# A decoder step with a mixture of experts: filled slots only, two-deep expert buffers, PLE weights split during the expert tiles

## The reference

```
xn = rmsnorm(h, g_ffn)
# top-1 of 4 groups, top-2 of its 8 experts, 32 experts in all
hg = silu(xn @ w_gate[e]) * (xn @ w_up[e])      # 1024 -> 256
y  = sum over the token's two experts of weight * (hg @ w_down[e])
h  = h + y
h  = h + sigmoid(rmsnorm(h, g_ple) @ w_ple_gate) * (p @ w_ple_proj)
out = rmsnorm(h, g_final)
```

## Time and profile before

| what | value |
|---|---|
| median of 3 runs | 1182.15 us (1180.9 to 1182.17) |
| profiled execution, span from first to last instruction | 1182.7 us |
| PE busy | 1075.1 us, 91% |
| DVE, ACT, POOL busy | 45%, 27%, 24% |
| DMA moved | 219.93 MB, mean 186 GB/s |
| gate/up matmuls, L1839 | 264.9 us busy |
| down matmuls, L1850 | 133.2 us busy |

### The profile page before, as it was taken

How to read it: one execution, slowest core, us unless ns; L and a number is a source line. 1 busy time by engine, 2 the same in 40 slices (tenths; PEclk the granted TensorE clock), 3 DMA queues, 4 the chain that set the end, 5 groups by cost and what they waited for, 6 DMA issues and landing times.

```text
span 1182.7 us, 13729 instructions
## 1 busy us (share of the span) xinstructions
PE 1075.1 (91%) x4696; PEld 573.2 (48%) x4696; DVE 534.8 (45%) x678; ACT 319.1 (27%) x573; POOL 279.3 (24%) x287
## 2 busy tenths in 40 slices
PE   4899979999999789995299999999999999589996
PEld 3556535555555555553144444444444444244442
DVE  6169856777765864344511211112111121356663
ACT  7342223222234433231011111111111111335553
POOL 0577235566415211110110100101010010232200
PEclk9999989989998799997599999999999999889998
DMA  7446610000004312228369999999999897743311
GB/s 254 129 154 219 131 4 1 1 0 0 0 1 124 113 44 99 71 71 308 114 253 360 370 369 366 375 363 369 370 359 380 328 350 275 255 125 116 115 45 58
DMA packets 50425, 219.93 MB, mean 186 GB/s; under 512 B 13569, under 2 KB 14866, under 8 KB 40146
## 3 DMA queue, kind: packets, MB, share of 16 engines
q1 hardware_dynamic: 42466, 190.58, 44.7%
q0 software_dynamic: 7920, 28.84, 7.3%
HBM read 180.44 MB, written 38.96 MB: 186 GB/s over the span
## 4 chain that ended last, share of the span: by engine, by line
PE 75%; DVE 11%; DMA 5%; ACT 3%; issue 2%; POOL 1%; DVEq 1%; SPq 0%; ACTq 0%; POOLq 0%
PE psum L1839 21%; PE psum L1614 12%; PE psum L1850 10%; PE psum L1925 8%; PE psum L1757 8%; DVE arena L1194 6%; PE psum L1830 3%; PE psum L1915 2%; DMA arena<-in_w_gu 2%; PE psum L1799 1%; PE psum L1681 1%; PE psum L1680 1%; PE psum L1790 1%; PE psum L1684 1%; PE psum L1669 1%
## 5 line engine op out<-in xcount | busy, mean ns | idle before, releaser
L1839 PE MATMUL psum<-arena 128*128 128x512 f32 x592 | 264.9, 601 | 4.0 <-DMA arena<-in_w_gu 2.8
L1194 DVE SCALAR_TENSOR_TENSOR arena<-arena,wc x120 | 185.3, 1544 | 17.4 <-DVE arena L1194 17.0
L1839 PEld LDWEIGHTS psum<-arena 128*128 128x128 f32 x592 | 111.1, 193 | 131.7 <-issue 126.4
L1614 PE MATMUL psum<-arena 128*128 128x512 f16 (+1 forms) x864 | 153.7, 332 | 0.6 <-ACT arena L887 0.6
L1850 PE MATMUL psum<-arena 128*128 128x512 f32 x296 | 133.2, 593 | 1.0 <-DVE arena L1488 1.0
L1484 DVE TENSOR_TENSOR arena<-arena,psum 128x256 f32<-128x256 f32 x37 | 15.6, 421 | 249.0 <-ACT arena L1057 211.5
L1614 PEld LDWEIGHTS psum<-arena 128*128 (+1 forms) x864 | 68.3, 98 | 78.6 <-issue 9.5
L1606 PE MATMUL psum<-arena 128*128 128x384 f16 x576 | 96.8, 332 | 4.0 <-DVE arena L1161 2.4
L1757 PE MATMUL psum<-arena 128*128 128x512 f16 x432 | 98.7, 386 | 0.8 <-DVE arena L1322 0.8
L1925 PE MATMUL psum<-arena 128*128 128x512 f16 x432 | 96.5, 383 | 2.5 <-DVE arena L1543 2.5
L787 POOL COPY idx<-ids 128x1 int32 (+1 forms) x32 | 6.3, 196 | 322.0 <-PE psum L1830 262.6
(11 more groups left out here) (232 smaller groups left out, 1231.1 us busy)
## 6 DMA issues: line engine op xcount, KB each, us to landing
arena<-in_w_gu SPq DMA_DIRECT2D x37, 2048.0 KB, 8.6
arena<-in_w_dn SPq DMA_DIRECT2D x37, 1024.0 KB, 10.5
yrows<-arena SPq DMA_DIRECT2D x37, 512.0 KB, 3.5
yrows<-PT SPq DMA_DIRECT2D x2, 4096.0 KB, 19.4
side<-in_w_tok SPq DMA_DIRECT2D x16, 388.0 KB, 3.4
arena<-in_x SPq DMA_DIRECT2D x9, 512.0 KB, 4.2
side<-in_x SPq DMA_DIRECT2D x9, 512.0 KB, 4.0
xn<-arena SPq DMA_DIRECT2D x9, 512.0 KB, 2.9
```

The source lines that it names most:

```text
L1194: dve.scalar_tensor_tensor(acc, src, w[:, k:k + 1], acc, ALU.mult, ALU.add).then_inc(conv, 1)
L1614: x = pe.matmul(out, xnT[w][:, k, bass.ds(n * P, P)], wtok[m][:, k, col:col + width], start=k + w + m == 0, stop=k == KC - 1 and w == 1)
L1839: x = pe.matmul(psum[:, 2 + sl, :], xgT[sl][:, k, :], wgu[sl][:, k, :], start=k == 0, stop=k == KC - 1)
```

## The change

- `experts` takes a second function `between`, called after tiles 0 to 3 and 28 to 31; tiles 4 to 27 run in a loop of two.
- Weights, gathered rows, transposed rows and results have two buffers instead of three. Gate/up comes in two halves with a semaphore each. SP asks for gate/up of t+2 when gate_up(t) is done and for down of t behind that.
- The one-hot matmul carries token+1, negative for a second choice, so that an empty slot shows as 0. DVE makes `ids` and `idsY` from it; an empty slot's index is out of bounds and its row is left out (slot 0 of an empty tile keeps an index, to a spare row). The gather buffers are cleared once by POOL.
- POOL gathers four tiles ahead in its list and scatters results with an indirect DMA straight to row token + m x 1152 of `yrows`. SP then loads result rows directly (`load_y`) instead of POOL gathering them.
- Only the 64 padding rows of each half of `yrows` are zeroed, not the extra tiles.
- The eight chunks of the PLE gate weight are loaded and split after tiles 0 to 3 and 28 to 31.
- Many small tiles move to one scratch tensor `tmp`, part of which is reused by these weights and results.

The diff, cut to its core:

```diff
-    put("token", token * (token < SEQ + NS))
+    put("token", (token + 1) * (token < SEQ + NS))
+    put("empty", np.concatenate([np.where(s == 0, TOK - 1, NOROW), np.where(s == 0, 2 * TOK, NOROW)], 1) + 1)
...
+def experts(eng, body, between):
+
+
+    for t in range(NE):
+        if t == 4:
+            with eng.Fori(2, NE // 2 - 2) as i:
+                body(2 * i, 0)
+                body(2 * i + 1, 1)
+        elif not 4 <= t < NE - 4:
+            body(t, t % 2)
+            between(t if t < 4 else t - NE + KC)
...
-    return t // 3 if isinstance(t, int) else (t - s) // 3
-
-
-def extra_turn(t, s):
-
-    return 16 * ((NE + 2 - s) // 3) + 8 * (t - (2 - s)) + 16
+    return 8 * (t - s) + 16
...
+        wgu = [at(R3 + 4096 * j, KC, 2 * FF) for j in range(2)]
+        wdn = [at(R4 + 2048 * j, FC, D) for j in range(2)]
+        xg = [at(R3 + 8192, D), at(R4 + 4096, D)]
+        xgT = [at(RT + D * j, KC, P) for j in range(2)]
+        yt = [tat(D * j, D) for j in range(2)]
+        sil = [at(RT + 2048 + FF * j, FF) for j in range(2)]
+        hg = at(RT + 2048 + 2 * FF, FF)
+        hT = at(RT + 2048 + 3 * FF, FC, P)
...
+        wple = at(R1 + 8192, D)
+        wgate = [thalves(2048 + D * k, 1, D) if k < 4 else halves(R5 + D * (k - 4), 1, D) for k in range(KC)]
...
             sp.wait_ge(zero, 1)
-            for half in range(2):
-                sp.dma_start(a["yrows"][NE * P:NTILE * P, half * 512:(half + 1) * 512].rearrange("(t p) w -> p t w", p=P),
-                             PT[:].rearrange("p a b -> p (a b)").unsqueeze(1).to_broadcast([P, EXTRA, 512])
-                             ).then_inc(y_zero, 16)
+            for m in range(2):
+                sp.dma_start(a["yrows"][m * TOK + SEQ + NS:(m + 1) * TOK].rearrange("p (a b) -> p a b", b=512),
+                             PT[0:TOK - SEQ - NS].rearrange("p a b -> p (a b)").unsqueeze(1)
+                             .to_broadcast([TOK - SEQ - NS, 2, 512])).then_inc(y_zero, 16)
...
+            def load_gu(t, sl):
+                for u in range(2):
+                    if late(t, 2):
+                        sp.wait_ge(gu_ps, t - 1)
+                    sp.dma_start(wgu[sl][:, 4 * u:4 * u + 4, :], a["w_gu"][bass.ds(t, 1), :, 4 * u:4 * u + 4, :]
+                                 .rearrange("a p k f -> (a p) k f")).then_inc(gu_in[sl][u], 16)
+
+            def load_dn(t, sl):
+                if late(t, 2):
+                    sp.wait_ge(y_ps, t - 1)
                 sp.dma_start(wdn[sl], a["w_dn"][bass.ds(t, 1)].rearrange("a p k f -> (a p) k f")).then_inc(dn_in[sl], 16)
...
             sp.wait_ge(og_rdy, NT)
-            weights(1, 1)
+            load_gu(0, 0)
             xn2_store(NT - 1, 0)
-            sp.wait_ge(w_ps, 2 * NT)
-            weights(0, 0)
+            load_gu(1, 1)
             sp.wait_ge(lg_ps, NT)
-
+            load_dn(0, 0)
+            load_dn(1, 1)
...
+            def load_ple(k):
+                if k:
+                    sp.wait_ge(wl_lo, KC + k)
+                sp.dma_start(wple, a["w_ple"][:, k]).then_inc(wple_in, 16)
 
             def expert_io(t, sl):
-                y_store(t, sl)
-                weights(t + 3, sl)
-
-            with sp.Fori(0, (NE - 5) // 3) as i:
-                for sl in range(3):
-                    expert_io(3 * i + sl, sl)
-            expert_io(NE - 5, 0)
-            expert_io(NE - 4, 1)
-            y_store(NE - 3, 2)
+                if not isinstance(t, int) or t < NE - 2:
+                    load_gu(t + 2, sl)
+                else:
+                    with sp.If(count > t + 2 - NE):
+                        extra_gu(t + 2 - NE, sl)
+                if late(t, 2):
+                    load_dn(t, sl)
+
+            def extra_gu(t, sl):
+                e = sp.value_load(plan[0:1, bass.ds(t, 1)], min_val=0, max_val=NE - 1)
+                for u in range(2):
+                    sp.wait_ge(gu_ps, t + NE - 1)
+                    sp.dma_start(wgu[sl][:, 4 * u:4 * u + 4, :], a["w_gu"][bass.ds(e, 1), :, 4 * u:4 * u + 4, :]
+                                 .rearrange("a p k f -> (a p) k f")).then_inc(gu_in[sl][u], 16)
+
+            def extra_io(t, sl):
+                e = sp.value_load(plan[0:1, bass.ds(t, 1)], min_val=0, max_val=NE - 1)
+                sp.wait_ge(y_ps, t + NE - 1)
+                sp.dma_start(wdn[sl], a["w_dn"][bass.ds(e, 1)].rearrange("a p k f -> (a p) k f")).then_inc(dn_in[sl], 16)
+                with sp.If(count > t + 2):
+                    extra_gu(t + 2, sl)
+                hold(sp, passed)
...
+            experts(sp, expert_io, load_ple)
             extra(sp, count, extra_io)
-            for sl in range(3):
-                sp.wait_ge(y_out[sl], 16 * ((NE + 2 - sl) // 3))
-            sp.sem_inc(y_all, 1)
+
+            def load_y(n, j):
+                if late(n, 2):
+                    sp.wait_ge(add_rdy, 2 * n - 2)
+                for m in range(2):
+                    sp.dma_start(yg[j][m], a["yrows"][bass.ds(n * P + m * TOK, P), :]).then_inc(yg_in[j][m], 16)
+
+            sp.wait_ge(moe_done, 1)
+            sp.dma_start(wproj, a["w_proj"]).then_inc(pw_in, 16)
...
+                    load_y(2 * i + j + 2, j)
+                    load_p(2 * i + j + 2, j)
                     y_final(2 * i + j, j)
-                    load_p(2 * i + j + 2, j)
...
+            pl.wait_ge(og_rdy, NT)
+            pl.memset(xg[0], 0.0)
+            pl.memset(xg[1], 0.0).then_inc(zero, 1)
+            pl.wait_ge(zero, 4)
...
             def gather(t, sl):
-                if late(t, 3):
-                    pl.wait_ge(xgT_ps, t - 2)
+                if late(t, 2):
+                    pl.wait_ge(xgT_ps, t - 1)
                 pl.tensor_copy(idx[sl][:], ids[:, bass.ds(t, 1)]).then_inc(idx_rdy, 1)
                 pl.wait_ge(idx_rdy, t + 1)
                 hold(pl, passed)
-                pl.indirect_dma_start(xg[sl], None, a["xn2"], bass.IndirectOffsetOnAxis(idx[sl][:], 0)).then_inc(xg_in[sl], 16)
+                pl.indirect_dma_start(xg[sl], None, a["xn2"], bass.IndirectOffsetOnAxis(idx[sl][:], 0),
+                                      bounds_check=TOK - 1, oob_is_err=False).then_inc(xg_in[sl], 16)
+
+            def scatter(t, sl):
+                pl.wait_ge(y_a, t + 1)
+                pl.wait_ge(y_v, t + 1)
+                pl.tensor_copy(idy[sl][:], idsY[:, bass.ds(t, 1)]).then_inc(idy_rdy, 1)
+                pl.wait_ge(idy_rdy, t + 1)
+                hold(pl, passed)
+                pl.indirect_dma_start(a["yrows"], bass.IndirectOffsetOnAxis(idy[sl][:], 0), yt[sl], None,
+                                      bounds_check=2 * TOK, oob_is_err=False).then_inc(y_out[sl], 16)
+
+            def expert(t, sl):
+                if isinstance(t, int) and t >= NE - 4:
+                    with pl.If(count > t + 4 - NE):
+                        gather(t + 4, sl)
+                else:
+                    gather(t + 4, sl)
+                scatter(t, sl)
...
             gather(0, 0)
             gather(1, 1)
-            gather(2, 2)
-            with pl.Fori(1, (NE - 2) // 3) as i:
-                for sl in range(3):
-                    gather(3 * i + sl, sl)
-            gather(NE - 2, 0)
-            gather(NE - 1, 1)
+            pl.wait_ge(ids_rdy, 2)
+            pl.wait_ge(pos_rdy, 1)
...
+            def expert_extra(t, sl):
+                with pl.If(count > t + 4):
+                    gather(t + NE + 4, sl)
+                scatter(t + NE, sl)
+                pl.wait_ge(y_out[1 - sl], turn_of(t + NE - 1, 1 - sl))
                 hold(pl, passed)
-                pl.indirect_dma_start(xg[sl], None, a["xn2"], bass.IndirectOffsetOnAxis(idx[sl][:], 0)).then_inc(xg_in[sl], 16)
...
+            for sl in range(2):
+                pl.wait_ge(y_out[sl], 8 * NE)
+            pl.sem_inc(y_all, 1)
...
+            def split_ple(k):
+                act.wait_ge(wple_in, 16 * (k + 1))
+                act.activation(wgate[k][0][:, 0, :], wple, ACT.Copy).then_inc(wl_hi, 1)
...
-            act.wait_ge(wple_in, 16 * KC)
-            for k in range(KC):
-                if k == 3:
-                    act.wait_ge(y_all, 1)
-                if k >= 6:
-                    act.wait_ge(wl_lo, KC + k - 5)
-                act.activation(wgate[k][0][:, 0, :], wple[k], ACT.Copy).then_inc(wl_hi, 1)
...
-            step(dve.scalar_tensor_tensor(two["fy"], two["t"], float(P), two["r"], ALU.mult, ALU.add))
...
-            dve.tensor_copy(ids[:], psum[:, 2, 0:NTILE]).then_inc(ids_rdy, 1)
+            found = slots["found"]
+            step(dve.tensor_copy(found, psum[:, 2, 0:NTILE]))
+            dve.tensor_scalar(slots["none"], found, 0.0, None, ALU.is_equal)
+            step(dve.scalar_tensor_tensor(slots["abs"], found, -1.0, found, ALU.mult, ALU.max))
+            step(dve.tensor_scalar(slots["miss"], slots["none"], C["empty"][:, 0:1], -1.0, ALU.mult, ALU.add))
```

(82 more changed lines are left out.)

299 lines of the change are left out of this document (111 added, 188 removed).

## The result

The changed kernel takes **1212.65 us** (median of 4 runs, 1211.01 to 1214.37) against 1182.16 us before: 1.0258 times as long, 95% interval 1.0236 to 1.0279. The forecast was 1179.5, with a range up to 1194. The profiled execution's span is 1212.6 us against 1182.7.

The account below looks back on a forecast made before the run. The prediction took the PE to bound the kernel, never waiting in the expert loop. Its terms, +1 + 3 - 4.6 + 0.6 - 2.6 = -2.6 us, gave 1179.5 us from a median of 1182.15, range 1171.5 to 1194.

Parts of the forecast that it names:

- The step that failed: PLE stage: later tiles' loads behind y_final on SP are asked for early enough and cost 0.
- down late in the two-deep ring: Expert loop: down weights usually land 1.2 us early, two tiles 0.4 to 0.5 us late; +1 us charged.
- PLE splits in the expert tiles: Eight expert tiles: ACT waits for PLE weight loads with silu queued behind; tiles 0 and 1 free; +3 us.
- extra tiles: Five extra expert tiles: waits for gate/up weights and the slowed gate/up after them go; -4.6 us.
- routing: Before the first gather: DVE needs three or four more small operations in series for the indices; +0.6 us.
- passage: Last down projection to first PLE gate matmul: scatter and direct loads replace store and gathers; -2.6 us.
- zeroing, memsets: Dropped zeroing and POOL's two memsets of gather buffers: both hidden behind other work; 0.
- The first rival: Expert loop: down lands too late in most tiles; 17 us at halfway (1196), 68 at most; chance 0.15.
- the second rival: Expert tiles with splits: ACT held by PLE loads in all eight, 16 us instead of 3, 1192; chance 0.13.
- the rate that the prediction weighed: Expert loop: a skill page's 358 GB/s per core, giving +8 us for late down; set aside for the trace's 368.

Follow-up runs that it names:

- the first run: The changed kernel with SP's PLE-stage list shifted by one tile, result rows asked for one place further ahead of the store: 1185.62 us, 1.0015 times before.
- POOL's queue: The changed kernel with the direct loads of result rows issued by POOL instead of SP: 1186.39 us, 1.0012 times before.
- down-first run: The changed kernel with SP's PLE-stage list shifted by one tile and down of tile t asked for ahead of gate/up of t+2: 1179.28 us, 0.9951 times before.

## Why the prediction was wrong

**The step that failed** is "Later tiles' loads wait behind y_final on SP, but are asked for more than 10 us ahead of the transposes that need them: 0". The wait was seen, and its customer was the wrong one. The transposes of tile n+3 are indeed far off. But DVE's combine of n+3 and ACT's square of n+3 stand ahead of the finish of n+1 in lists that are as strict as SP's, and that finish is what the next load waits for, by way of its store. The prediction asked of every wait who stands behind it on the waiting engine, SP; it did not ask it of the engines that wait for SP. No rival had it either. The trace of before would have given most of the size: a landing of 4.2 us, then in series two steps of the combine, ACT's square and sigmoid and four steps of the finish, each 1.0 to 1.3 us, two table loads of 1.28 and 1.1 us of small steps. That is an estimate of 17.3 us without any hand-over between engines, against the PE's 14.7; the turn measured 19.0. **Term: 0; measured: about +29**, the stage's 30.0 less about 1 us that the first run keeps there, its first tile being longer at the PE's lower clock.

The other terms came out as follows (measured on the profiles; the first run stands for the change without the ring).

| term | forecast us | measured us |
|---|---|---|
| down late in the two-deep ring | +1 (0 to 68) | +0.8 in the first run, +0.4 with POOL's queue, +3.4 in the kernel after |
| PLE splits in the expert tiles | +3 (0 to 16) | +6.4 in the first run: 1.5 in tiles 0 and 1, 4.9 later |
| extra tiles | -4.6 | -5.0: 13.83 + 13.20 + 12.16 less 3 x 11.40 before, no DMA wait now |
| routing | +0.6 | +0.9: last router logits to first gate/up, 34.4 us (33.5 before) |
| passage | -2.6 (-7 to +3) | -3.0: 21.6 in the first run against 24.5; 21.4 in the kernel after |
| zeroing, memsets | 0 | nothing seen |

- **Down**: the mechanism was right; the size, forecast at +1, is 0.4 to 3.4 from profile to profile. Where the DMA queue is crowded it is late by up to 1.4 us, in few tiles, and the median tile is in time. The first rival (late in most tiles) did not happen.
- **PLE**: the mechanism was right, silu held by ACT's copy, and the second rival's 16 us too many. The size was half. Two things were missed: chunk 0 is in tile 0 not free, because without a down projection ahead of it silu of tile 1 is due sooner; and the later chunks land up to 12.5 us after their issue, beside down, gathers and scatters.
- **Passage**: the pieces came close. The scatter of 11 rows landed in 2.8 us (3.2 forecast), the walk took 2.4 (2.5), the second load landed 1.3 us behind the first (1).

Without the failed step the kernel stands at 1.0015 times before and not at the 0.998 that was forecast; the PLE splits make most of that. So a small gain was wrong as well, by about 4 us, while the order of two commands on one queue was worth 30.

## What to carry to other kernels

A prefetch that stands behind a store on the same queue is no prefetch: it starts when the tile before is finished, and if the consumers' own lists put the prefetched tile ahead of the current one's last steps, the two close into a ring whose length replaces the bottleneck's period. Follow such a wait around all the lists until it either ends at an engine with slack or comes back to where it began, and add up the loop. Ask first for the transfer whose buffer is free first, not for the one that was written first.

## What the runs showed of the hardware

**The PE's clock can change a profile by 2 us behind one and the same stall.** In the mixing stage the PE stalls 3.13 us for DVE. Granted clock between 440 and 450 us, first before, then after (columns as above):

```profile
440.00:450.00 10.00, 8.06 (x37) 5.57 (x37) 5.23 (x10) 3.11 (x13) 0.78 (x2) 0.66 0.43 131
```

```profile
440.00:450.00 10.00, 8.78 (x54) 5.69 (x55) 6.34 (x12) 5.10 (x19) 1.77 (x2) 1.00 0.31 105
```

Before, the clock fell to 1.2 GHz behind that stall, and eight transposes took 1.97 us and the next twelve matmuls 4.29; after, it stayed at 2.4 GHz and they took 1.09 and 2.75. Of the eight profiles of this study, five fell there and three did not. It makes 2.3 of the 3.2 us by which the stage ahead of the routing ended sooner in the profile after. The start of the routing moves by 5 us over the eight profiles (549.6 to 554.9), so a term of a few us is read inside its stage, not from where a stage begins.

**Stalls do not always cost what the clock then loses.** Behind the 4.00 us wait in the ring, eight matmuls of the projection took 6.29 us, at a granted clock of 0.51 between 1080 and 1085 us; at the full clock they take 3.62. It costs nothing there, since the ring runs through SP, DVE and ACT.

**DMA above the rate that the prediction weighed.** In the down-first run, between 600 and 605 us:

```profile
600.00:605.00 5.00, 5.00 (x13) 2.20 (x12) 0.00 (x0) 0.00 (x0) 0.32 (x1) 1.00 0.99 412
```

That is 412 GB/s with the DMA engines 99% busy. The Trainium skill, Perfetto Trace Analysis, section Roofline, says that the 358 GB/s are a core's share when both cores of a pair draw on the memory, and that one alone is bounded by its 16 DMA engines at some 435 GB/s; the row agrees, and the lower figure was no limit here.
